# The first feed-forward's stripes turned by the DMA crossbar, with another first load and another order around the norms

## What is computed

```python
def first_block(x, ...):
    h = rms_norm(x, pre_mix_g)
    a, gate, q, k, v = split(h @ w_in)
    yc = conformer_conv_group(a, gate, ...)          # GLU, depthwise conv, LayerNorm, swish
    ya = neighbourhood_attention_group(q, k, v, rpb)
    mix = concatenate([yc, ya]) @ w_out
    x = x + rms_norm(mix, post_mix_g)
    h = rms_norm(x, pre_mlp_g)
    f = square(relu(h @ w_up)) @ w_down              # 2048 -> 8192 -> 2048
    x = x + rms_norm(f, post_mlp_g)
    return x                                         # then second_block(x)
```

## Time and profile before

| | us |
|---|---|
| median of 3 runs | 2186.52 (2183.7 to 2187.66) |
| the profiled execution | 2183.4 |
| its span, first to last instruction | 2181.6 |
| TensorE busy | 2157.3 |
| VectorE busy | 1345.7 |
| ScalarE busy | 1078.5 |
| DMA, mean rate | 192 GB/s |

### The profile page before, as it was taken

One profiled execution on the slowest core, in us unless ns is written; L12 is line 12 of the kernel. 1 busy time (PEld: TensorE's weight loads), 2 busy tenths in 40 slices (PEclk: granted clock), 3 DMA queues, 4 the chain that ended last, 5 costly groups with the idle time before them and its releaser, 6 DMA issues.

```text
span 2181.6 us, 27377 instructions
## 1 busy us (share of the span) xinstructions
PE 2157.3 (99%) x9970; PEld 1786.6 (82%) x9970; DVE 1345.7 (62%) x1795; ACT 1078.5 (49%) x1500; POOL 59.1 (3%) x70
## 2 busy tenths in 40 slices
PE   8999999999999999999999999999999999999999
PEld 6888887888888888888878888888888888788887
DVE  5898857655555555555677545556445666666764
ACT  6545565654443444444565445554444555564442
POOL 0000100000000000000000000000000000000000
PEclk9999999999999999999999999999999999999999
DMA  9565446556666565666565765556666564555975
GB/s 321 183 187 166 144 154 209 186 185 192 210 186 195 187 190 187 191 186 192 175 195 193 213 192 178 177 175 185 203 201 201 175 192 141 168 174 177 326 239 164
DMA packets 117541, 419.90 MB, mean 192 GB/s; under 512 B 13208, under 2 KB 13472, under 8 KB 117152
## 3 DMA queue, kind: packets, MB, share of 16 engines
q1 hardware_dynamic: 115520, 412.10, 59.8%
q0 software_dynamic: 1744, 5.77, 0.9%
q10 hardware_dynamic: 144, 0.28, 0.0%
HBM read 407.60 MB, written 10.49 MB: 192 GB/s over the span
## 4 chain that ended last, share of the span: by engine, by line
PE 81%; DVE 2%; issue 0%; ACT 0%; POOL 0%; ACTq 0%; DVEq 0%
PE g L578 25%; PE g L580 25%; PE g L579 25%; PE s L557 2%; PE s L798 0%; PE s L797 0%; DVE wlo L1429 0%; DVE ta_lo L1604 0%; PE s L805 0%; DVE arena L1597 0%; PE s L673 0%; ACT whi L897 0%; PE s L739 0%; PE s L740 0%; PE s L738 0%
## 5 line engine op out<-in xcount | busy, mean ns | idle before, releaser
L1429 DVE TENSOR_TENSOR wlo<-raw,whi 128x1024 fp32r<-128x1024 f32 x734 | 894.4, 1223 | 607.9 <-ACT whi L897 606.2
L897 ACT ACTIVATE whi<-raw 128x1024 fp32r<-128x1024 f32 x734 | 773.1, 1058 | 663.7 <-PE g L580 655.1
L578 PE MATMUL g<-whi,ta_hi 128*128 128x512 f32 x1920 | 764.6, 398 | 11.5 <-DVE wlo L1429 9.2
L580 PE MATMUL g<-whi,ta_lo 128*128 128x512 f32 x1920 | 749.7, 390 | 0.0
L579 PE MATMUL g<-wlo,ta_hi 128*128 128x512 f32 x1920 | 748.2, 390 | 0.0
L578 PEld LDWEIGHTS g<-whi,ta_hi 128*128 128x128 f32 x1920 | 361.2, 188 | 84.9 <-issue 13.2
L580 PEld LDWEIGHTS g<-whi,ta_lo 128*128 128x128 f32 x1920 | 360.7, 188 | 77.1
L579 PEld LDWEIGHTS g<-wlo,ta_hi 128*128 128x128 f32 x1920 | 361.6, 188 | 71.7
L578 PE MATMUL g<-whi,tb_hi 128*128 128x512 f32 x1008 | 399.0, 396 | 0.2 <-ACT arena L1079 0.2
L580 PE MATMUL g<-whi,tb_lo 128*128 128x512 f32 x1008 | 393.1, 390 | 0.0
L579 PE MATMUL g<-wlo,tb_hi 128*128 128x512 f32 x1008 | 392.5, 389 | 0.0
(11 more groups left out here) (216 smaller groups left out, 914.9 us busy)
## 6 DMA issues: line engine op xcount, KB each, us to landing
raw<-in_w_in SPq DMA_DIRECT2D x320, 512.0 KB, 4.1
raw<-in_w_up SPq DMA_DIRECT2D x128, 512.0 KB, 3.6
raw<-in_w_down SPq DMA_DIRECT2D x128, 512.0 KB, 3.5
raw<-in_w_out SPq DMA_DIRECT2D x64, 512.0 KB, 4.0
raw<-in_w_a SPq DMA_DIRECT2D x32, 512.0 KB, 4.3
raw<-in_w_b SPq DMA_DIRECT2D x32, 512.0 KB, 4.5
raw<-in_w_ukv SPq DMA_DIRECT2D x16, 512.0 KB, 4.1
raw<-in_w_uq SPq DMA_DIRECT2D x12, 512.0 KB, 3.6
```

The costliest lines, as they stand in the source:

```text
L578: e.matmul(o, xh, wh, start=first, stop=False)
L580: ins = e.matmul(o, xl, wh, start=False, stop=last)
L897: e.activation(whi[u % RING][:, 0:n], raw[u % RAW][:, 0:n], ACT.Copy).then_inc(s_hi, 1)
L1429: e.tensor_tensor(l, r, h.bitcast(F32), ALU.subtract).then_inc(s_lo, 1)
```

## The change

1. **Turning through the crossbar.** TensorE's `up_side` is gone. At `E + 1` VectorE copies the squared stripe into `PL`, the 16-bit halves of its words apart (two copies). At `E + 4` SP issues four `dma_start_transpose`, one for each half and tile, of 128 rows with 512 16-bit elements, into `PT`. At `E + 10` VectorE waits for them (`d_turn`) and puts the halves together again in `UZ` (two copies). At `E + 12` ScalarE writes `tb_hi` from `UZ`, at `E + 13` VectorE `tb_lo`. `PL`, `PT` and `UZ` lie where `GN` is, which the feed-forward doesn't use.
2. **First load.** Units 0 and 1 are loaded, split and waited for in halves, and x block by block. ScalarE's queue loads the first block of x and the 16 columns of `pre_mix_g`; the rest of the table comes later on SP's. One ScalarE instruction on zeros stands ahead of all others, and five matmuls on zeros ahead of the dense ones on TensorE.
3. **Norms.** Where two stripes are last, the first is finished and squared a unit earlier; the gain of a slice that is needed late is taken behind the additions of the slices needed first; the transposes of the first two slices of a tile come half a slot later; and `low` of six units behind each norm is moved back by 1 to 4 slots.
4. **Attention.** On VectorE `at_side` stands ahead of the `uqr`, `uqn`, `ukn` sides, and the second half's rotary work at `E + 4` and `E + 8`, not 2 and 5.

The diff, cut to its core:

```diff
@@ slots_and_splits
+            behind = {b + m: n for b in HEAD for m, n in ((3, 1), (4, 4), (5, 2), (6, 2), (7, 2), (8, 2))}
-                at.setdefault(slot + late * (v - 3 in HEAD or v - 4 in HEAD), []).append(v)
+                at.setdefault(slot + late * behind.get(v, 0), []).append(v)
@@ buffers
+        def words(v):
+            return v.bitcast(I16).rearrange("p (n h) -> p h n", h=2)
+        PL = ar(14576, 1024).bitcast(I16).rearrange("p (h t n) -> p h t n", h=2, t=2)
+        PT = ar(15600, 1024).bitcast(I16).rearrange("p (h c n) -> p h c n", h=2, c=4)
+        UZ = ar(16624, 1024)
@@ pe
-            def up_side():
-                for i in range(16):
-                    for pair in range(2):
-                        yield E(f"up{i // 2}{i % 2}") + 3 + pair
-                        k = 2 * i + pair
-                        b = bank(k % 4, (up_h, k + 1), (up_l, k + 1))
-                        q.wait_ge(up_s, i + 1)
-                        turn(b, SG[i % 4], pair).then_inc(up_t, 1)
...
+            q.wait_ge(dve_own, 1)
+            for n in (256, 256, 256, 256, 128):
+                e.matmul(sps[3][:, 0:n], junk[:, 0:P], junk[:, 0:n], start=True, stop=True)
...
                 for t, c, slot in NORM_TURNS:
-                    yield 2 * b + slot
+                    yield 2 * b + slot + (c == 0) / 2
@@ act, up_side
-                    for pair in range(2):
-                        yield E(st.name) + 3 + pair
-                        k, c = 2 * i + pair, i // 2
-                        q.wait_ge(up_t, k + 1)
-                        q.wait_ge(s_mm, mm_of("mixc3" if c == 0 else "mixq3" if c == 1 else f"down{c - 2}3"))
-                        turn_hi(tb_hi, 8 * (c % 2) + 4 * (i % 2) + 2 * pair, k % 4).then_inc(up_h, 1)
+                    yield E(st.name) + 12
+                    c = i // 2
+                    q.wait_ge(up_w, 2 * i + 2)
+                    q.wait_ge(s_mm, mm_of("mixc3" if c == 0 else "mixq3" if c == 1 else f"down{c - 2}3"))
+                    for pair in range(2):
+                        kt = 8 * (c % 2) + 4 * (i % 2) + 2 * pair
+                        e.activation(tb_hi[:, kt:kt + 2, :], UZ[:, 512 * pair:512 * pair + 512].rearrange("p (k n) -> p k n", k=2),
+                                     ACT.Copy).then_inc(up_h, 1)
@@ act, start
-            e.dma_start(VC[:, :], d["vec"]).then_inc(d_vec, 16)
+            e.dma_start(XT[:, 0, :], d["xt"][:, 0, :]).then_inc(d_x0, 16)
+            e.dma_start(vec("pre_mix_g", 0, 16), d["vec"][:, 0:16]).then_inc(d_gain0, 16)
+            q.wait_ge(dve_own, 1)
+            e.activation(junk[:, 256:257], junk[:, 0:1], ACT.Copy)
@@ dve, norm_side
                 def root(t):
                     q.wait_ge(squared[0], squared[1] + len(last) * (t + 1))
                     mean_of_tile(ss_of, t, names[1] + str(t))
-                    q.wait_ge(added[0], added[1] + len(last) * (t + 1))
-                    for n in last:
-                        gained[0] = gain(n, (t,))
...
+                if two_last:
+                    yield 2 * b - 7
+                    finish(0, 0)
                 yield 2 * b - 5
-                finish(0)
+                finish(0, end)
+                if two_last:
+                    gained_last(0, 0)
                 root(0)
+                gained_last(0, end)
...
+                yield 2 * b + 7
+                gained_last(1, end)
                 add(1, 3)
@@ dve, up_side
-                    for pair in range(2):
-                        yield E(st.name) + 3 + pair
-                        k = 2 * i + pair
-                        q.wait_ge(up_h, k + 1)
-                        turn_lo(tb_hi, tb_lo, 8 * (i // 2 % 2) + 4 * (i % 2) + 2 * pair, k % 4).then_inc(up_l, 1)
+                    yield E(st.name) + 1
+                    q.wait_ge(up_s, i + 1)
+                    q.wait_ge(d_turn, 64 * i)
+                    for h in range(2):
+                        e.tensor_copy(PL[:, h], words(STG[i % 4][:, :])[:, h].rearrange("p (t n) -> p t n", t=2)).then_inc(up_p.sem, 1)
+                    yield E(st.name) + 10
+                    q.wait_ge(d_turn, 64 * i + 64)
+                    q.wait_ge(up_h, 2 * i)
+                    q.wait_ge(up_l, 2 * i)
+                    for h in range(2):
+                        e.tensor_copy(words(UZ)[:, h].rearrange("p (c n) -> p c n", c=4), PT[:, h]).then_inc(up_w.sem, 1)
+                    yield E(st.name) + 13
+                    for pair in range(2):
+                        kt = 8 * (i // 2 % 2) + 4 * (i % 2) + 2 * pair
+                        q.wait_ge(up_h, 2 * i + pair + 1)
+                        q.wait_ge(up_w, 2 * i + 2)
+                        e.tensor_tensor(tb_lo[:, kt:kt + 2, :], UZ[:, 512 * pair:512 * pair + 512].rearrange("p (k n) -> p k n", k=2),
+                                        tb_hi[:, kt:kt + 2, :].bitcast(F32), ALU.subtract).then_inc(up_l, 1)
@@ dve, uqr_side
-                        yield E(f"uqr{hf}") + 2 + 3 * t
+                        yield E(f"uqr{hf}") + ((2, 5), (4, 8))[hf][t]
@@ sync
+            def turn_side():
+                for i in range(16):
+                    yield E(f"up{i // 2}{i % 2}") + 4
+                    q.wait_ge(up_p, 2 * i + 2)
+                    q.wait_ge(up_w, 2 * i)
+                    for h in range(2):
+                        for t in range(2):
+                            e.dma_start_transpose(PT[:, h, :, t * P:(t + 1) * P], PL[:, h, t]).then_inc(d_turn.sem, 16)
...
-            for p in range(4):
+            load_half(0, 0)
+            e.dma_start(XT[:, 1, :], d["xt"][:, 1, :]).then_inc(d_xt[0], 16)
+            load_half(0, 1)
+            load_xt(1)
+            load_half(1, 0)
+            load_half(1, 1)
+            for p in range(2, 4):
                 load_xt(p)
                 load(p)
+            e.dma_start(vec("pre_mlp_g", 0, NVEC - 16), d["vec"][:, 16:NVEC]).then_inc(d_vec, 16)
```

More of the change, by code:

```diff
@@ L332, in two_blocks @@
         d_xt = [sem(f"d_xt{i}") for i in range(8)]
+        d_gain0, d_x0 = sem("d_gain0"), sem("d_x0")
+        d_half = [sem(f"d_half{i}") for i in range(2)]
         d_cst, d_vec, d_pos, d_xr, d_pg, d_pg2, d_x2s, d_rows, d_f2 = (sem(n) for n in (
@@ L821, in ao_side @@
                         q.wait_ge(at_x, 4 * n + 4)
-                        turn(b, ZB[n % 2], pair).then_inc(ao_t.sem, 1)
+                        turn(b, ZB[n % 2], pair).then_inc(ao_t, 1)
             def y_side():
@@ L844, in pe @@
                                 dense(u + i, j, (t,))
-                            for g in sides:
-                                g.upto(2 * u + 4 * t + i)
+                                for g in sides:
+                                    g.upto(2 * u + 4 * t + i - (j == 0) / 2)
                     u += 4
@@ L1410, in act @@
                 for u in units:
-                    split(u)
+                    if u >= 2:
+                        split(u)
             for g in sides:
@@ L1616, in norm_side @@
                 low_of(0, 0)
-                yield 2 * b - 1
-                finish(1)
+                for m in range(len(last)):
+                    finish(1, m)
+                yield 2 * b - 2
                 low_of(0, 1)
@@ L1628, in norm_side @@
                 low_of(1, 1)
+                if two_last:
+                    gained_last(1, 0)
                 add(1, 2)
@@ L2076, in dve @@
                 for u in units:
-                    low(u)
+                    if u >= 2:
+                        low(u)
             for g in sides:
```

168 lines of the change are left out of this document (94 added, 74 removed).

## The result

The changed kernel takes **2161.66 us** (median of 4 runs, 2161.0 to 2163.23), the kernel before, run beside it, 2185.26 (4 runs, 2183.7 to 2187.66): a ratio of 0.9891, 95% interval 0.9876 to 0.9907. The forecast was 2160.7, range 2151 to 2178. It was right within 1 us, but not because its terms were right: their sum was 4.0 us too high, and an offset of about 3 us between the profiled execution and the median, which the forecast added to it, hid most of that.

The account below looks back on a forecast made before the run. TensorE, busy 2157.3 of 2181.6 us, was taken as the bound. Turns 14.8, start 4.5, norms 4.5 and attention 2.0 sum to 25.8 us, off the 2186.5 median: 2160.7 us, range 2151 to 2178.

Parts of the forecast that it names:

- The turns: Feed-forward: 32 turns of 0.46 us leave TensorE, which never waits there, so 14.8 us come off.
- VectorE: Feed-forward: four added copies per stripe at 1.2 us each, 77 us in all, 69% busy, hidden at cost zero.
- The 8.6 us of slack: Feed-forward: a weight's low part is made four units (10.9 us) ahead of its use, less 2.3 us for ScalarE and VectorE.
- The crossbar: Feed-forward: four DMAs per stripe land in 4 to 10 us without stalling TensorE; slow-crossbar rival up to 2316 us, chance 0.13.
- The stall bound of 13.4 us: Feed-forward: TensorE stalls only if the four crossbar DMAs land later than 13.4 us after their issue.
- Each microsecond beyond costs 16: Feed-forward: each microsecond the crossbar DMAs land past the stall bound costs 16 us over the kernel.
- The start: Before and just after the first matmul: 3.6 us earlier, 1.4 from the clock, less 0.5 for weights; 4.5 us (3 to 5.5).
- I take 4.0: Start: x, gains and weights for the first half unit have landed at 4.0 us, giving the first matmul at 5.6.
- the gain in clock: Start: five matmuls on zeros ahead of the dense ones bring back 1.4 us lost to the lower clock level.
- The term for the third unit's weights: Start: the third unit's weights are used at 11.0 us and ready at 11.2, so 0.5 us is taken off.
- The norms: Both norms: reordering VectorE work and TensorE transposes removes 4.5 of 6.4 us of gaps (bounds -1 to 6.4).
- The attention: Second block's attention: its subtraction goes ahead of VectorE's rotary work, removing 2.0 us (0 to 2.5) of a 2.5 us wait.

Follow-up runs that it names:

- Experiments 3 and 4: 3: crossbar_8 and crossbar_12. 4: changed kernel with each of the four VectorE copies of the turning made three times; 2175.68 us, ratio 0.9958.
- crossbar_8: Changed kernel with eight crossbar DMAs per stripe instead of four, the extra ones written to a place nobody reads; 2170.05 us, ratio 0.9931.
- crossbar_12: Changed kernel with twelve crossbar DMAs per stripe, the last four issued only when the first eight have landed; 2282.86 us, ratio 1.0447.
- gains_first_warm_long: Changed kernel with 8.5 instead of 4.5 warm-up products on zeros and the gains loaded ahead of the first x block; 2162.63 us, ratio 0.9893.
- turns_on_tensor: Changed kernel with only the turning put back on TensorE; 2177.17 us, ratio 0.9963.
- warm_long: Changed kernel with 8.5 instead of 4.5 warm-up products of 256 columns on zeros; 2162.41 us, ratio 0.9891.
- xbar_alone: Kernel before with only the crossbar turning put in, start, norms and attention as before; 2173.09 us, ratio 0.9943.
- attention_as_before: Changed kernel with VectorE's attention side behind the rotary work again and rotary work at 2 and 5 slots; 2164.54 us, ratio 0.9901.

## Why the prediction came out

**The turns: right.** 14.8 us were taken off, 15.2 measured, and nothing took their place on TensorE. The 0.4 is the rounding of 0.68 us per triple.

**VectorE: right for the wrong price.** A copy costs 0.69 or 0.75 us, not 1.2 (the row was of 32-bit words; the lower bound, half of it, was the near one), so 2.7 us per stripe and 62% busy instead of 69%. The 8.6 us of slack was worked out for each stripe by itself. Experiments 3 and 4 show that what is late in one `up` stripe is handed on through ScalarE to the next, so that the third and fourth of the four in a row have less. In the changed kernel nothing is handed on (0.4 us at all 16), and so the step did no harm.

**The crossbar: right.** The four took 6.3 to 7.6 us from issue, inside the 4 to 10 taken. The stall bound of 13.4 us becomes 24.5 - 1.2 - 1.4 - 6.5 = 15.4 after the issue with the measured copies and issue time, for a stripe that begins on time. It fits there within 0.3 us: 11.6 to 12.4 us (crossbar_8) stalled nothing, and 17.9 to 19.4 (crossbar_12) stalled for 2.7 to 4.2. "Each microsecond beyond costs 16" was too kind: crossbar_12 is 3.0 beyond on average, which should give 48 us and gave 121, as the second stripe of a pair inherits a delay and the clock falls with the gaps.

By the 261 GB/s of the Trainium skill, DMA: Bandwidth & Descriptors, section on latency and other measured facts, 512 KB would take 2 us, as an estimate. By the 1309 ns per 128x128 block of the Trainium skill, VectorE: DVE Perf Modes, section on the three transpose paths, sixteen blocks in a row would take 20.9 us, as an estimate. The trace agrees with neither as a rate: 16 blocks in 6.7 us are 0.42 us a block, and SP's queue alone needs 5.1 us to issue them; one DMA of four blocks landed in 3.3 us.

**The start: the step that failed.** 4.5 us expected, 2.1 measured. Of the difference 1.2 is the first dense matmul (6.82, not 5.6): the data term "I take 4.0" went by the amount of data, where the last piece needed, the gains, was there at 4.97 (+1.0; of this 0.27 hangs on their place in the queue, as gains_first_warm_long shows, and what holds back the rest is open), and halves cost a little more than half (0.51 + 0.61 + 0.69 for 0.45 + 0.53 + 0.62, +0.2). The other 1.1 lies behind the first dense matmul, where 1.4 - 0.5 = 0.9 were expected and -0.2 measured by the 97th: the gain in clock was taken off as certain, and in this execution the clock fell after the 2 us gap between warm-up and first product. In turns_on_tensor, where it held, this part is the 0.9 expected. The term for the third unit's weights, "needed 11.0, ready 11.2", was sound in kind and 2 us too small: ready at 13.3 in warm_long, where it ate 1.1 of the 1.6 us that the clock gave.

**The norms: the other step that failed.** 4.5 expected, 2.2 measured. The working, 1.28 + 0.7 of the 2.12 us at one tile, is what happened there: it fell to 0.22. The error was to take the listed waits for the whole cost and to give 0.7 us to "most of the others". The delays came back as smaller pieces, most of 0.35 to 0.45 us and in the list with 0.2 or not at all, the longest of 0.65 us (listed as 0.49), where a product waits for `ta_lo`; at the second norm they give back everything. The bounds, -1 to 6.4, held it.

**The attention:** 2.0 expected, 2.3 measured; nothing was late in its place.

**From the profiled execution to the median.** The terms gave 25.8 us, and executions without a fall of the clock differ by 20.3 + 1.6 = 21.9: 2183.4 - 21.9 = 2161.5, which is where three of the four runs of the changed kernel lie (2161.0, 2161.68, 2161.64; their mean granted clock is 1.000). The fourth, 2163.23 at 0.998, is the profiled one with its fall. The forecast added 3.1 us to 2157.6, since the profiled execution before lay that far under the median. That offset did not carry over; by luck it filled most of the hole of 4.0. Runs of the kernel before come in two groups, 2183.4 to 2184 and 2186.1 to 2187.7. The mean granted clock stands beside the time of 24 of them: 1.000 in all 7 of the lower group, 0.999 or 0.998 in all 17 of the upper. So the offset of 3.1 us goes with a lower clock in the runs that the median stands for. Behind which waits it fell in them no trace shows, as none of an upper run exists; that the change, by taking some of these waits away, makes such falls rarer is argued and not shown.

## What to carry to other kernels

On an engine that is never idle over a stage, instructions taken off it are worth their distance from start to start, one for one, as long as the replacement lands inside the slack of the buffer ring; compute that bound in time before, look for pieces that follow each other so closely that an engine in strict order hands the delay of one on to the next, and expect a steep loss beyond it. Short waits are better summed from start to start than from the list of waits, which leaves out what is shorter than the modelled tail of a matmul. And when forecasting from one profiled execution, don't add its distance to the median without asking what makes that distance.

## What the runs showed of the hardware

- A crossbar DMA of 128x512 16-bit words holds SP's queue for 1.26 us (1.19 to 2.4), against 0.33 for most plain loads of 512 KB, and lands 3.3 us after issue in the median (2.5 to 5.5). Here the issues, not the bytes, set the pace.
- VectorE copies 128x1024 words of 16 bits in 0.69 us with every second word as source, and in 0.75 with every second word as destination; 32-bit operations of that shape take 1.22.
- Behind the same gap of TensorE, in the same or nearly the same program, the granted clock sometimes fell to its lower level for 3 to 4 us and sometimes not: 2.0 us at 260 us (fell in 3 of 12 traces, the kernel before not among them), 2.5 us at the attention (fell in xbar_alone, neither before nor in attention_as_before), 1.2 to 2.0 us after the short warm-up (lower level in 3 traces, upper in 4). At the first two a fall cost 1.6 us.
- A small load isn't there sooner for being small: 8 KB in 64-byte rows, issued at 1.16 us behind 128 KB on the same queue, were waited for until 4.97; issued ahead of them, the 128 KB were the later piece, at 4.70.
